# Two of a pair's four weight sums added by accumulating DMAs instead of VectorE

## The reference, cut to what matters

```python
def swiglu(h, w_gate_up, w_down):
    g, u = jnp.split(h @ w_gate_up, 2, axis=-1)
    return (jax.nn.silu(g) * u) @ w_down
...
        x = x + swiglu(rmsnorm(x, ffn_norm[i]), ffn_w_gate_up[i], ffn_w_down[i])
```

## Time and profile before

| | us |
|---|---|
| median of 3 runs (2324.81 to 2325.91) | 2325.38 |
| the profiled execution | 2326.84 |
| its span, first to last instruction | 2325.0 |

### The profile page before, as it was taken

The page is one execution under the profiler, slowest core; times in us unless marked ns, Lnnn a source line. Parts: engine busy times, 40 slices in busy tenths (PEclk is TensorE's granted clock), DMA queues, the critical chain, the costliest instruction groups (busy, mean ns, idle before and its releaser), DMA issues.

```text
span 2325.0 us, 37973 instructions
## 1 busy us (share of the span) xinstructions
PE 2313.3 (99%) x14360; PEld 2078.9 (89%) x14360; DVE 1737.7 (75%) x2847; ACT 1131.9 (49%) x1944; POOL 308.1 (13%) x305
## 2 busy tenths in 40 slices
PE   9999999999999999999999999999999999999998
PEld 7889988999988889999988899998889998899997
DVE  8667668876965679687777897696756776978693
ACT  6268744544543335454533454454326783454453
POOL 2211140000030120000123000003320114000003
PEclk9999999999999999999999999999999999999999
DMA  4820013333323233333233333332470003223332
GB/s 160 220 64 2 1 56 100 114 96 102 114 84 102 89 108 100 99 109 110 78 97 100 99 111 100 95 116 84 123 209 28 1 2 98 89 93 102 98 101 84
DMA packets 69295, 217.38 MB, mean 93 GB/s; under 512 B 8193, under 2 KB 8321, under 8 KB 69121
## 3 DMA queue, kind: packets, MB, share of 16 engines
q1 hardware_dynamic: 62928, 204.39, 27.7%
q0 software_dynamic: 5184, 8.40, 1.8%
q10 hardware_dynamic: 1008, 2.21, 0.3%
HBM read 204.48 MB, written 2.10 MB: 89 GB/s over the span
## 4 chain that ended last, share of the span: by engine, by line
PE 77%; DVE 0%; ACT 0%; issue 0%; DVEq 0%; ACTq 0%
PE bank L1901 76%; PE bank L2241 2%; PE bank L2271 0%; DVE branch L1666 0%; DVE big L1894 0%; ACT L695 0%; DVE w_lo L1245 0%; ACT w_hi L737 0%; ACT xg L1108 0%; DVE act_t L1398 0%; DVE x L1208 0%; DVEq L255 0%; DVE rden L1661 0%; DVE rden L1663 0%; PE bank L2145 0%
## 5 line engine op out<-in xcount | busy, mean ns | idle before, releaser
L679 ACT ACTIVATE w_hi<-raw 128x1024 fp32r<-128x1024 f32 (+4 forms) x260 | 239.6, 922 | 297.0 <-DMA raw<-stream 238.3
L1141 DVE TENSOR_TENSOR w_lo<-raw,w_hi 128x1024 fp32r<-128x1024 f32 (+4 forms) x257 | 287.9, 1126 | 112.8 <-ACT w_hi L679 112.4
L1901 PE MATMUL bank<-hid_hi,w_hi 128*128 128x512 f32 x720 | 280.9, 390 | 0.0
L1901 PE MATMUL bank<-hid_lo,w_hi 128*128 128x512 f32 x720 | 280.5, 390 | 0.0
L1901 PE MATMUL bank<-hid_hi,w_lo 128*128 128x512 f32 x720 | 280.3, 389 | 0.0
L1901 PE MATMUL bank<-xs_hi,w_hi 128*128 128x512 f32 (+2 forms) x720 | 279.2, 388 | 0.8 <-DVE w_lo L1141 0.5
L1901 PE MATMUL bank<-xs_lo,w_hi 128*128 128x512 f32 (+2 forms) x720 | 273.4, 380 | 0.0
L1901 PE MATMUL bank<-xs_hi,w_lo 128*128 128x512 f32 (+1 forms) x704 | 267.5, 380 | 0.0
L1208 DVE TENSOR_TENSOR x<-bank,x 128x512 f32<-128x512 f32 (+1 forms) x160 | 110.2, 689 | 198.7 <-PE bank L1901 198.3
L1901 PE MATMUL bank<-mix_hi,w_hi 128*128 128x256 f32 (+1 forms) x768 | 246.0, 320 | 0.0
L1901 PE MATMUL bank<-mix_hi,w_lo 128*128 128x256 f32 (+1 forms) x768 | 244.8, 319 | 0.0
(11 more groups left out here) (280 smaller groups left out, 5878.8 us busy)
## 6 DMA issues: line engine op xcount, KB each, us to landing
raw<-stream SPq DMA_DIRECT2D x131, 512.0 KB, 3.7
raw_b<-pairs SPq DMA_DIRECT2D x80, 512.0 KB, 4.8
raw_a<-pairs SPq DMA_DIRECT2D x64, 512.0 KB, 4.6
raw<-stream SPq DMA_DIRECT2D x32, 448.0 KB, 3.4
raw<-stream SPq DMA_DIRECT2D x32, 384.0 KB, 3.1
raw<-stream SPq DMA_DIRECT2D x32, 320.0 KB, 2.9
w_f<-stream SPq DMA_DIRECT2D x18, 512.0 KB, 3.7
raw<-stream SPq DMA_DIRECT2D x34, 256.0 KB, 2.6
```

Of the source, the lines that this page charges most:

```text
L679: nc.scalar.activation(w_hi[:, slot, 0:n], raw[:, k, 0:n], ACT.Copy).then_inc(w_hi_ready, 1)
L1141: nc.vector.tensor_tensor(w_lo[:, slot, 0:n], raw[:, k, 0:n], f32(w_hi[:, slot, 0:n]), ALU.subtract).then_inc(w_lo_ready, counted(b))
L1901: return nc.tensor.matmul(out_, w, v, start=start, stop=stop, skip_group_check=onto)
```

## The change

The signs in Winograd's scheme are turned so that all four weight sums are pure additions. Two of them are then left to DMAs issued by GpSimd that add to their destination:

- SyncE loads each pair with a third DMA of 256 KB: quarter 3 once more, into a buffer `s1_of(j)` (two halves of the first part of `s32`). For the first pair of part 1 this waits until the norm's row is ready.
- GpSimd, in `weight_sums`, waits until the three loads of a pair have landed and issues two accumulating DMAs of 256 KB from DRAM: quarter 2 onto `s1_of(j)` (gives s1) and quarter 0 onto quarter 3 of the raw buffer (gives s3). They signal `sum_full`.
- VectorE waits for `sum_full` (both sums) in place of `pair_full`, and makes only s2 and s4.
- The chunks change places: c0 is now s1 (512 columns), c3 is a22 and s3 (1024 columns). ScalarE waits for `sum_full` ahead of c0 and c3.
- The hidden tiles of parts 1 to 3 come out negated, so x minus the bank is taken; two of the token sums become scalar_tensor_tensor.

```diff
-WEIGHT_AT = {"s3": (0, 0), "s1": (0, 512), "s2": (1, 0), "s4": (1, 512), "a11": (2, 0), "a12": (2, 512), "a22": (3, 0)}
+WEIGHT_AT = {"s1": (0, 0), "s2": (1, 0), "s4": (1, 512), "a11": (2, 0), "a12": (2, 512), "a22": (3, 0), "s3": (3, 512)}
...
             def load_pair(l, p, j):
...
+                if (p, j) != (1, 0):
+                    load_s1(l, p, j)
+
+            def load_s1(l, p, j):
+
+                q = pair_at(l, p, j)
+                sp.dma_start(s1_of(j), pairs[q, :, 3 * S:4 * S]).then_inc(pair_full[j % 2], 16)
...
+            def weight_sums(l):
+
+                for p in range(1, len(PARTS)):
+                    for j in range(PAIRS[p]):
+                        q = pair_at(l, p, j)
+                        gp.wait_ge(pair_full[j % 2], 48 * (loads_before(q) + 1))
+                        gp.dma_start(s1_of(j), pairs[q, :, 2 * S:3 * S], accum_op=ALU.add).then_inc(sum_full[j % 2], 16)
+                        gp.dma_start(pair_raw(j)[:, 3 * S:4 * S], pairs[q, :, 0:S], accum_op=ALU.add
+                                     ).then_inc(sum_full[j % 2], 16)
...
                 squares(norm_of_ffn(l))
+                weight_sums(l)
                 squares(norm_of_ffn(l) + 1)
...
             def pair_high(l, p, j, c):
...
-                if c < 2:
-                    act.wait_ge(s_ready, 3 * q + (1, 3)[c])
+                if c == 1:
+                    act.wait_ge(s_ready, 2 * q + 2)
                 elif c == 2:
-                    act.wait_ge(pair_full[j % 2], 32 * (loads_before(q) + 1))
+                    act.wait_ge(pair_full[j % 2], 48 * (loads_before(q) + 1))
+                else:
+                    act.wait_ge(sum_full[j % 2], 32 * (loads_before(q) + 1))
...
-                dve.wait_ge(pair_full[j % 2], 32 * (loads_before(q) + 1))
+                s1, s2, s4 = s1_of(j), s32[:, 2 * S:3 * S], s32[:, 3 * S:4 * S]
+                dve.wait_ge(sum_full[j % 2], 32 * (loads_before(q) + 1))
                 if q:
                     dve.wait_ge(sw_lo_ready, 4 * q - 2)
-                both = raw_q[:, :].rearrange("p (i c) -> p i c", i=4)
-                nc.vector.tensor_tensor(s32[:, 0:BW].rearrange("p (i c) -> p i c", i=2),
-                                        both[:, 3:4, :].broadcast_to([P, 2, S]), both[:, 0:3:2, :], ALU.subtract
-                                        ).then_inc(s_ready, 1)
...
+                nc.vector.tensor_tensor(s2, s1, a11, ALU.add).then_inc(s_ready, 1)
+                dve.wait_ge(s_ready, 2 * q + 1)
+                nc.vector.tensor_tensor(s4, a12, s2, ALU.add).then_inc(s_ready, 1)
...
-                        add_residual(k, b, slot)
+                        dve.wait_ge(block_done, b + 1)
+                        nc.vector.tensor_tensor(tile(x, k), tile(x, k), bank[slot][:, :], ALU.subtract
+                                                ).then_inc(taken, 1)
```

More of the change, by code:

```diff
@@ L426, in build @@
         pair_full = [sem("pair_full_b"), sem("pair_full_a")]
+        sum_full = [sem("sum_full_b"), sem("sum_full_a")]
         scaled_ready, t_ready, t_hi_ready, t_lo_ready, b_hi_ready, b_lo_ready = (sem(n) for n in (
@@ L438, in chunk, with s1_of @@
         def chunk(l, p, j, c):
+            n = S if c == 0 else BW
             if pair_slot(p, j):
-                t = (xs_hi, xs_lo)
-                hi, lo = (a[:, 2 * c:2 * c + 2, :].rearrange("p a t -> p (a t)") for a in t)
+                at = MT - 2 if c == 0 else 2 * c - 2
+                hi, lo = (a[:, at:at + n // S, :].rearrange("p a t -> p (a t)") for a in (xs_hi, xs_lo))
             else:
                 slot = (plan.ffn[l] + c) % RING
-                hi, lo = w_hi[:, slot, :], w_lo[:, slot, :]
-            return (hi[:, 0:S], lo[:, 0:S]) if c == 3 else (hi, lo)
+                hi, lo = w_hi[:, slot, 0:n], w_lo[:, slot, 0:n]
+            return hi, lo
         def chunk_from(j, c):
-            if c < 2:
-                return s32[:, bass.ts(c, BW)]
-            return pair_raw(j)[:, 0:BW] if c == 2 else pair_raw(j)[:, BW:BW + S]
+            if c == 0:
+                return s1_of(j)
+            return s32[:, BW:2 * BW] if c == 1 else pair_raw(j)[:, bass.ts(c - 2, BW)]
+        def s1_of(j):
+            return s32[:, bass.ts(j % 2, S)]
         def plain_before(l, p):
@@ L546, in load_pair @@
                 q = pair_at(l, p, j)
-                if j % 2 and j == 1:
+                if j == 1:
                     sp.wait_ge(w_lo_ready, plain_before(l, p))
+                    sp.wait_ge(sw_lo_ready, 4 * (q - 1))
                 elif j > 1:
@@ L561, in _ @@
                 load_pair(l, 1, 0)
-                loads(up + 4, up + 2 * FIRST_TILES + MT)
+                loads(up + 4, up + 2 * FIRST_TILES)
+                sp.wait_ge(row_ready, norm_of_ffn(l) + 1)
+                load_s1(l, 1, 0)
+                loads(up + 2 * FIRST_TILES, up + 2 * FIRST_TILES + MT)
                 for p in range(1, len(PARTS)):
@@ L1227, in pair_sums @@
                 a11, a12 = raw_q[:, 0:S], raw_q[:, S:BW]
-                s3, s1, s2, s4 = (s32[:, bass.ts(i, S)] for i in range(4))
-                dve.wait_ge(pair_full[j % 2], 32 * (loads_before(q) + 1))
+                s1, s2, s4 = s1_of(j), s32[:, 2 * S:3 * S], s32[:, 3 * S:4 * S]
+                dve.wait_ge(sum_full[j % 2], 32 * (loads_before(q) + 1))
                 if q:
                     dve.wait_ge(sw_lo_ready, 4 * q - 2)
-                both = raw_q[:, :].rearrange("p (i c) -> p i c", i=4)
-                nc.vector.tensor_tensor(s32[:, 0:BW].rearrange("p (i c) -> p i c", i=2),
-                                        both[:, 3:4, :].broadcast_to([P, 2, S]), both[:, 0:3:2, :], ALU.subtract
-                                        ).then_inc(s_ready, 1)
[L1236 to L1239, removed]
+                nc.vector.tensor_tensor(s2, s1, a11, ALU.add).then_inc(s_ready, 1)
+                dve.wait_ge(s_ready, 2 * q + 1)
+                nc.vector.tensor_tensor(s4, a12, s2, ALU.add).then_inc(s_ready, 1)
             def pair_low(l, p, j, c):
@@ L1275, in token_sum @@
                     to = [t32[:, r, :, :].rearrange("p k t -> p (k t)") for r in range(4)]
-                    one, two, op, before = ((b12, b11, ALU.subtract, 0), (b22, to[0], ALU.add, 1),
-                                            (b22, b12, ALU.add, 0), (b21, to[1], ALU.subtract, 2))[i]
+                    before = (0, 1, 0, 2)[i]
                     dve.wait_ge(scaled_ready, MT * l + (4 if i == 0 else MT))
@@ L1280, in token_sum @@
                         dve.wait_ge(t_ready, 4 * l + before)
-                    nc.vector.tensor_tensor(to[i], one, two, op).then_inc(t_ready, 1)
+                    if i % 2 == 0:
+                        nc.vector.tensor_tensor(to[i], (b11, None, b22)[i], b12, ALU.subtract).then_inc(t_ready, 1)
+                    else:
+                        nc.vector.scalar_tensor_tensor(
+                            out=to[i], in0=b22 if i == 1 else to[1], scalar=-1.0, in1=to[0] if i == 1 else b21,
+                            op0=ALU.mult, op1=ALU.subtract).then_inc(t_ready, 1)
                 def token_low(i):
```

1 line of the change is left out of this document (removed).

## The result

| | before | after |
|---|---|---|
| median, us | 2325.28 | 2473.02 |
| lowest to highest, us | 2324.81 to 2325.91 | 2470.56 to 2475.74 |
| span of the profiled execution, us | 2325.0 | 2473.9 |
| TensorE busy, us | 2313.3 | 2354.4 |
| TensorE not busy, us | 11.7 | 119.5 |

The ratio is 1.0635, 95% interval 1.0617 to 1.0654: 148 us slower, where 59 were forecast; the time lies just inside the upper end of the stated range (2475). The table splits the 148.9 us of span: 107.8 us are time in which TensorE has nothing to do, 41.1 us are the same 14360 matmuls taking longer. VectorE's busy time did fall, by 82 us.

A forecast was written before the change was run, and what follows sets the result against it. TensorE was taken as the bound, 99% busy. Stalls of 1.9 + 7.2 + 5.6 = 14.7 us a layer, 58.8 in four layers, on 2325.4 gave 2384 us, 2.5% slower; range 2330 to 2475.

The forecast's parts named there:

- the chain: Part 2: pair 1's sums land, VectorE's queued work, pair 2 loaded 3.2 us later, its sums land, then TensorE's s3 starts.
- the clusters: TensorE waiting at s3 of pair 0 in part 1, s4 or s3 of pair 1 in parts 2 and 3; twelve in all.
- GpSimd's issue is held up by VectorE: Rival: VectorE, busy 97% of the time there, delays GpSimd's DMA issue; left inside the range, no chance of its own.
- C: Time from SyncE's first load of a pair to the landing of both accumulating DMAs: 11.3 us, ends 8.8 and 14.3.
- loads: From SyncE's first issue for a pair until its third load lands: 5.2 us, between 5.0 and 5.6.
- second issue: On GpSimd, the second accumulating DMA goes out 0.8 us after the first, between 0.5 and 1.05.
- landing: Accumulating DMA from issue to landing: 4.2 + 1.1 = 5.3 us, between 3.3 and 7.7.
- C - 9.4, 2C - 15.4 and 2C - 17.0: TensorE's stalls per layer at the first pairs of parts 1, 2 and 3: 1.9, 7.2 and 5.6 us.
- the loop: Sums landed, 7.7 us of VectorE's way to the next load, then C; two pairs allow 20.16 us, binding from C = 12.4.
- Hidden chain: Rival: accumulating DMAs land so fast that C is under 7.7 and no stall is left; 2325 us, chance 0.10.
- short landings: Rival: 256 KB lands in 2.6 us, C is 8.6, stalls 8 us in all; 2333 us, chance 0.14.
- Slow accumulation: Rival: the two DMAs don't overlap or adding costs more than a second read; C 15 to 16, 2528 us, chance 0.12.

## Why the prediction was wrong in size

*Right.* VectorE's lost work is worth nothing: 82 us less of it (88 said) and no gain. VectorE and ScalarE wait in order, TensorE behind them; in part 2 of layer 0 each step of the chain is within 0.1 us of the prediction's. TensorE's idle time before its first matmul of s4 or s3 is longest where the prediction put the clusters: in layer 0, in part 1 3.0 + 1.2 us, in part 2 1.2 + 8.1, in part 3 7.4. That GpSimd's issue is held up by VectorE could be left inside the range, as it was: the two issues stand 0.54 us apart in the median, at most 1.07.

*Wrong: the size of C*, 11.3 forecast, 13.9 measured. By term:

| term | forecast | measured | what the runs showed |
|---|---|---|---|
| loads | 5.2 | 6.6 | the third load lands 5.3 us after its own issue, not 4.4: +0.83; beside accumulating DMAs another +0.5 |
| GpSimd's wake | not counted | 0.3 | |
| second issue | 0.8 | 0.54 | as its copies of 64 partitions |
| landing | 5.3 | 5.7 | 3.4 without adding, 4.3 by itself |

The four measured terms give 13.1; C's own median is 13.9, since loads and landings both have slow cases far above their medians, in different pairs (their means are 6.9 and 6.2). The worst term is the loads: I gave the third load's landing as between 5.0 and 5.6 after the first issue by its size alone, as if the queue ahead of it were empty. The landing came out near its forecast, but by a wrong road: I scaled GpSimd's 128 KB copies (4.2 us), while a plain 256 KB needs 3.4 and adding makes up the rest.

*C counts five times a layer.* Stalls were C - 9.4, 2C - 15.4 and 2C - 17.0. At 13.93 they are 4.5 + 12.5 + 10.9 = 27.9 a layer, 111 us, against 58.8. And the loop binds from 12.4: 13.93 + 7.7 - 20.16 = 1.5 us at four or five places a layer, 24 to 29 us. In all 135 to 141 of the 148; the prediction's own upper end, C = 14.3, gave 147. The traces split the 148.9 us in the same way, 114 at the starts and 34 in later pairs, and so do the kernels with other C. So the mechanism holds with its terms put right, and the step that failed is the first one: the terms of C, the loads above all (5.2 forecast, 6.6 measured). That the one median gives the starts so well has some luck in it: with the C of each place the three stalls are 104 us, and the clock adds the rest.

*Wrong: one C for all pairs.* It runs from 11.9 to 18.2. In pair 1 it is 15.2 us in part 1, in the mean of the four layers, but 12.5 in part 2 and 12.2 in part 3. In part 1 pair 2 is loaded in the same moment in which pair 1's sums go out (queue of SyncE; GpSimd), and the second DMA needs 8.6 us:

```profile
411.99 0.80 SPq L561 DMA_DIRECT2D raw_b<-pairs  x2
```
```profile
413.00 1.19 POOL L661 DMA_DIRECT2D raw_a<-pairs  x1
```

Where loads and accumulating DMAs meet, the loop loses time in the middle of a part too (in layer 0 single waits of 0.5 to 0.8 us in part 1 and 3.1 in part 3; in layer 3 5.0), where the prediction said "none elsewhere". It had named this sign itself: TensorE stalls beyond the starts if C is over 12.4.

*Not foreseen: the clock.* The sum has no term for it. TensorE's matmuls took 41 us more. Not all of it is lost time, but TensorE falls 15 us further behind after the start of s3 (11 in the first two pairs, 4 in the later ones), where it has no wait left: these stand in the 148. Another part lies just ahead of it, as s3 above started 0.5 us after its operands were ready. They are no clean price of the clock, though: where 11.5 us of the busy time were taken away, the time stayed (within the scatter of these runs), since the later pairs waited longer. What the kernel would take at the full clock was not settled.

*The rivals.* Hidden chain and short landings are out: C never falls under 11.9. The rule of the Trainium skill for a GpSimd DMA (DMA: Bandwidth & Descriptors, section "Anatomy of one DMA — SWDGE (gpsimd) path") made 256 KB an estimated 2.6 us; here even plain ones take 3.2 to 3.4, accumulating ones 4.2 to 5.7, and the measurement decides. Slow accumulation is half true. The two do overlap, so C isn't 15 to 16, but adding costs 1.0 and 2.2 us. Whether that is the second read, which is all that the Trainium skill has the adding step of a ReduceScatter pay for (Collectives: The Full Stack, section "The bandwidth ceiling: the fold count and why AG ≠ RS ≠ AR"), or more than it, no run here tells: none times a DMA that reads twice and doesn't add. Of the 1.0 us some 0.3 are no read, since they pass before the first packet.

*Still open* is also how much of the dearer adding is the second read and how much the smaller packets.

## What to carry to other kernels

An engine that is nearly full but for which the bound engine hardly waits has nothing to give when it is relieved; what counts is how late the new path delivers. Put a DMA chain in front of an in-order wait only where the time from "buffer free" to "first use" is longer than the whole chain (loads behind each other, wake, issue, landing, all under the load of their neighbours), and count its length twice where the next buffer's load stands behind that same wait. And where a second engine is 97% busy, as VectorE was, there are nearly two bounds: 0.6 us more a pair for VectorE cost 0.4 us a pair.

## What the runs showed of the hardware

- Adding makes a GpSimd DMA of 256 KB 1.0 us longer (3.2 to 4.2) when it is the first of two, 2.2 us (3.4 to 5.7) when it is the second; one by one both take 4.3. It also moves its bytes in packets of 2 KB, the plain DMA in packets of 4 KB.
- The second of two accumulating DMAs takes 5.5 us in the median with no load of SyncE beside it, 6.9 beside a pair's loads and 6.6 beside the plain stream's (at most 5.9, 8.6 and 8.7).
- A 256 KB load behind two of 512 KB lands 5.2 to 5.3 us after its issue, alone it took 2.6.
- Two accumulating DMAs of 128 partitions go out 0.54 us apart on GpSimd, hardly more than its 64-partition copies took (0.525).
- After TensorE had stood 8.07 us its granted clock was at the low level, and a matmul of 256 columns took 0.21 us instead of 0.12.
- Two VectorE sums of 512 columns in place of one of 1024, with the chunks' new places, cost this kernel 14.7 us in 72 pairs, and more of it by waits for ScalarE than by VectorE's own work.
